# Second layer without the leading tokens behind its S5 input and rows, and S5 states stored from a copy

## Chip, cores and metric

The kernel runs on one core of a Trainium2 chip, as one launch. The metric is the device time of an execution in microseconds. The core's engines are TensorE (PE in the profile, PEld for its weight loads), VectorE (DVE), ScalarE (ACT), GpSimd (POOL) and SyncE (SP); all transfers run on 16 DMA engines, whichever engine's queue issues them.

## The reference

One inference step of a decoder with two layers over 280 columns: 16 learned leading tokens, 256 prompt tokens and 8 sample tokens (one step for each of 8 sequences with old states). The leading tokens are dropped from the result. All data are float32.

```python
for l in range(2):
    proj = rmsnorm(x) @ w_in[l]      # S5 input (512) | RWKV rows (1792) | two gates (1024 each)
    ya, xr, xi = s5_branch(proj[..., :512], ...)        # diagonal complex scan, GELU, GLU
    yb, s_fin, sh = rwkv7_branch(proj[..., 512:2304], ...)
    m = sigmoid(gate_a) * ya + sigmoid(gate_b) * yb
    x = x + m @ w_out[l]
    x = x + (swiglu(rmsnorm(x)) if l == 0 else moe(rmsnorm(x)))   # top 2 of 8 experts
y = rmsnorm(x)[:, 16:]
```

Besides y, the last S5 states, the RWKV states and the last projected rows of both layers are returned, for the prompt and for each sample sequence. A layer's scans need the leading tokens of that layer's S5 input and RWKV rows. In the second layer nothing else of these tokens reaches a result.

## The kernel before

Activations lie with the feature on the partitions and T = 280 columns (N_META = 16 leading ones, TP = 272 with the prompt, then NS = 8 samples). x, h and gate are [128, chunk, T]; each 128-wide output tile of a matrix product goes to one PSUM bank as 128 x 280. All weights come in one stream of 1 MB slots through a ring of seven, which SP refills in order as TensorE gives slots back (weights_used).

Each engine runs one program written out by hand, and engines meet by semaphores alone. For layer l TensorE's mix (L1051) does: the norm's sums; 12 tiles of RWKV rows; the S5 input matrices (b_turned, direct); the last two row tiles and four tiles of S5 input; then the S5 inputs (inputs), the low-rank products (lora), and the 16 gate tiles (proj_tile with n of at least CR + CA = 18), the later ones mixed with kk_sums, bonus_sums and four y5_tile calls. y5_tile makes the S5 output of one chunk from the scanned states xs by many small products; it shares one bank, so each waits for VectorE's y5_add of the one before. Then rwkv interleaves sixteen halves of the GLU (glu_half, 4 products each) with the chunked RWKV-7 solve. finish_rwkv (L1005 on) does the group norm, the eight w_bo tiles, the eight w_out tiles and the sums of the next norm. One float32 product appears in the records as two matmuls.

ScalarE evicts every projection tile (proj_out: identity for rows and S5 input, sigmoid for the gates). After the gate tile with n = 30 it runs the exponentials of the cumulative decay, the GELU and the last three sigmoids. The exponentials write beta and kr, which lie on the bytes of xs. VectorE runs the scan (scan), then the RWKV inputs with bonus_in at L1853, and y5_add.

POOL's queue stores the last S5 states: column 68 of xs (the prompt) and columns 69 to 76 (the samples), 9 floats in a run, 32 runs in each partition.

```python
pool.wait_ge(S["scan_done"], l + 1)
pool.dma_start(a["o_s5"][l], xs[:, :, :, NK:XW]).then_inc(S["s5_out"], 16)
pool.wait_ge(S["so_out"], CB * (l + 1))
```

and ScalarE waits for that store ahead of its exponentials (`ac.wait_ge(S["s5_out"], 16 * (l + 1))`). After the second layer's mixer come the routing and the eight experts (TensorE gets split float32 products, weights split by ScalarE and VectorE), then the last norm (norm with i = 4) and the store of y in four DMAs on SP's queue.

Of the kernel before, what the change touches and what calls it, by code (L numbers as in the profile page):

```python
# [8 lines left out]
ALU = mybir.AluOpType  # L9
# [135 lines left out]
def build(nc, a, debug=None):  # L145

    with ExitStack() as ctx:
# [37 lines left out]
        rstd = sb("rstd", [P, 2, T])  # L185
        wend = sb("wend", [P, CB, 1 + NCH + NS])
# [75 lines left out]
        names = ["x_in0", "x_in1", "ones_in", "first_in", "consts", "small_w", "s0_in", "shift_out", "s5_out", "rw_out", "y_stored",  # L262
# [64 lines left out]

        def quad(bank, n):
            return pools[bank][:, 0:256 * n].rearrange("p (f t) -> p f t", f=CB * n)
# [9 lines left out]
        def _(sp):  # L339
# [35 lines left out]
        def _(pool):  # L375
# [34 lines left out]
            for l in range(DEPTH):  # L410
# [16 lines left out]
                pool.dma_start(a["o_s5"][l], xs[:, :, :, NK:XW]).then_inc(S["s5_out"], 16)  # L427
# [17 lines left out]
        def _(pe):  # L445
# [20 lines left out]
            def norm(i):  # L466


                for c in range(DC):
                    pe.wait_ge(S["norm_sq"], DC * i + c + 1)  # L470
                    last = mm(pools[0][:, 0:T], ones[:], squares(i)[:, c, :], c == 0, c == DC - 1)
                    if c == 0 and i in (1, 3):
                        last.then_inc(S["weights_used"], 1)
                last.then_inc(S["norm_ps"], 1)

            def proj_tile(l, n, at):
# [16 lines left out]
                products(pools[n % 3][:, 0:T], [(w[:, j, k, :], h[:, k, :]) for k in range(DC)], "proj_ps",  # L493
# [71 lines left out]
            def glu_half(l, n, c):  # L565
# [14 lines left out]
                products(pools[bank][:, 0:T], [(w[:, n % 2, c, k, :], y5[:, k, :]) for k in range(CA)],  # L580
# [424 lines left out]
            def finish_rwkv(l):  # L1005
# [5 lines left out]
                for f in range(CB):  # L1011
                    mm(pools[f][:, 0:T], blk[:], o_t[:, f, :]).then_inc(S["gn_ps"], 1)
                for f in range(CB):
                    pe.wait_ge(S["o_sq"], CB * l + f + 1)
                    last = mm(pools[4][32 * f:32 * f + 32, 0:T], blk[:, 0:P:4], tmp[1][:, f, :])
                last.then_inc(S["gn_ps"], 1)
                pe.wait_ge(S["gn_dve"], (2 * CB + 1) * l + CB + 1)
                for f in range(CB):
                    q = slice(32 * f, 32 * f + 32)
                    mm(pools[4 + f][:, 0:T], spread[q, :], rstd[q, 1, :]).then_inc(S["gn_ps"], 1)  # L1020
                base = MIX_AT[l] + S_WIN + S_GLU
                for n in range(DC):
# [6 lines left out]
                    if n == 0:  # L1029
                        for k in range(CB):  # L1030
                            pe.wait_ge(S["gn_dve"], (2 * CB + 1) * l + CB + k + 2)
                            last = mm(pools[0][:, 0:T], w[:, 0, k, :], o_t[:, k, :], k == 0, k == CB - 1)
                        last.then_inc(S["bo_ps"], 1)
                    else:
                        products(pools[n % 4][:, 0:T], [(w[:, n % 4, k, :], o_t[:, k, :]) for k in range(CB)], "bo_ps",
# [4 lines left out]
                for n in range(DC):  # L1040
# [6 lines left out]
                    products(pools[4 + n % 4][:, 0:T], [(w[:, n % 2, k, :], gate[:, k, :]) for k in range(DC)], "wo_ps",  # L1047
# [232 lines left out]
        def _(ac):  # L1280
# [9 lines left out]
            def norm(i):  # L1290
# [3 lines left out]
                for c in range(DC):  # L1294
# [6 lines left out]
                    fn(squares(i)[:, c, :], x[:, c, :], ACT.Square).then_inc(S["norm_sq"], 1)  # L1301
# [5 lines left out]
                fn(rstd[:, 0, :], pools[0][:, 0:T], ACT.Sqrt, scale=1.0 / D, bias=eps[:, 0:1]).then_inc(S["norm_rt"], 1)  # L1307

            def proj_out(l, n):
# [6 lines left out]
                else:  # L1316
                    ins = fn(gate[:, n - CA - CR, :], src, ACT.Sigmoid)
# [15 lines left out]
            def mix(l):  # L1333
# [46 lines left out]
                ac.wait_ge(S["s5_out"], 16 * (l + 1))  # L1380
# [12 lines left out]
                for f in range(CB):  # L1393
                    ac.wait_ge(S["gn_dve"], (2 * CB + 1) * l + f + 1)
                    fn(tmp[1][:, f, :], o_t[:, f, :], ACT.Square).then_inc(S["o_sq"], 1)
                ac.wait_ge(S["gn_ps"], (2 * CB + 1) * l + CB + 1)
                fn(rstd[:, 0, :], pools[4][:, 0:T], ACT.Sqrt, scale=1.0 / N, bias=eps[:, 1:2]).then_inc(S["o_std"], 1)
# [6 lines left out]
            def glu_gate(l, n):  # L1404
# [4 lines left out]
                fn(glu_s[:, n % 2, :], pools[4 if n else 5][:, 0:T], ACT.Sigmoid).then_inc(S["glu_sig"], 1)  # L1409
# [253 lines left out]
        def _(dve):  # L1663
# [19 lines left out]
            def norm(i, gains, out):  # L1683
                dve.wait_ge(S["norm_rt"], i + 1)
                step(v.reciprocal(rstd[:, 1, :], rstd[:, 0, :]))  # L1685
                for c in range(DC):
                    ins = v.scalar_tensor_tensor(out=out[:, c, :], in0=x[:, c, :], scalar=gains[:, c:c + 1],  # L1687
                                                 in1=rstd[:, 1, :], op0=ALU.mult, op1=ALU.mult)
# [136 lines left out]
            def mix(l):  # L1825
# [70 lines left out]
                for f in range(CB):  # L1896
                    dve.wait_ge(S["gn_ps"], (2 * CB + 1) * l + f + 1)
                    stt(out=o_t[:, f, :], in0=pools[f][:, 0:T], scalar=-1.0 / N, in1=o_t[:, f, :],
# [5 lines left out]
                v.reciprocal(rstd[:, 1, :], rstd[:, 0, :]).then_inc(S["gn_dve"], 1)  # L1904
                for f in range(CB):
                    dve.wait_ge(S["gn_ps"], (2 * CB + 1) * l + CB + f + 2)
                    ins = stt(out=o_t[:, f, :], in0=o_t[:, f, :], scalar=col(l, "gn_g", f), in1=pools[4 + f][:, 0:T],
                              op0=ALU.mult, op1=ALU.mult)
                step(ins)
                for f in range(CB):  # L1910
                    ins = tt(o_t[:, f, :], o_t[:, f, :], bonus[:, f, :], ALU.add)
                step(ins)
                for f in range(CB):
                    tt(o_t[:, f, :], o_t[:, f, :], gg[:, f, :], ALU.mult).then_inc(S["gn_dve"], 1)  # L1914

                for n in range(DC):
                    dve.wait_ge(S["bo_ps"], DC * l + n + 1)
                    step(tt(gate[:, DC + n, :], gate[:, DC + n, :], pools[n % 4][:, 0:T], ALU.mult))
                    tt(gate[:, n, :], gate[:, n, :], gate[:, DC + n, :], ALU.add).then_inc(S["bo_out"], 1)
                for n in range(DC):  # L1920
                    dve.wait_ge(S["wo_ps"], DC * l + n + 1)
                    tt(x[:, n, :], x[:, n, :], pools[4 + n % 4][:, 0:T], ALU.add).then_inc(S["wo_out"], 1)
# [11 lines left out]
            def glu_out(l, n):  # L1934

                dve.wait_ge(S["glu_sig"], DC * l + n + 1)
                step(v.tensor_tensor(gate[:, n, :], gate[:, n, :], glu_s[:, n % 2, :], ALU.mult))
                dve.wait_ge(S["glu_value_ps"], DC * l + n + 1)
                v.tensor_tensor(gate[:, n, :], gate[:, n, :], pools[4][:, 0:T], ALU.mult).then_inc(S["glu_out"], 1)
# [554 lines left out]
OUTS = {"y": (P, DC, T), "o_shift": (DEPTH, P, CR, 1 + NS), "o_s5": (DEPTH, P, JT, 2, 1 + NS),  # L2494
# [3 lines left out]
def results(r):  # L2498
    y = r["y"].transpose(2, 1, 0).reshape(T, D)
# [5 lines left out]
    return (c(y[None, N_META:TP]), c(y[TP:, None]), c(s5[0, :, :1]), c(s5[1, :, :1]), c(rw[:, :1]), c(sh[:, :1]),  # L2505
# [17 lines left out]
```

## Time and profile before

| | |
|---|---|
| median of 3 runs | 2017.32 us (2012.21 to 2017.56) |
| profiled execution, own time | 2021.26 us |
| its span, first to last instruction | 2019.5 us |
| TensorE busy, mean granted clock | 96% of the span, 0.96 |
| VectorE, ScalarE, POOL busy | 66%, 48%, 2% |
| layer 0, its FFN, layer 1 up to its S5 inputs | 0 to 690 us |
| layer 1, gate tiles with scan and y5 | 690 to 783 us |
| layer 1, GLU, RWKV solve, tail, routing | 783 to 994 us |
| experts and combination | 994 to 2003 us |
| last norm and store | 2003 to 2019.5 us |

Times in the profile are microseconds from the span's start. A timeline row has start, duration, engine, line, operation and tiles (most of SBUF's tiles lie in one tensor, arena, and all PSUM tiles are called bank), the count of merged instructions (x16), and in brackets the engine's idle time ahead of it and what ended it. L447 is the helper through which every matmul is issued, L1282 that of every ScalarE operation. Ends of matmuls are modelled.

### The profile page before, as it was taken

How to read it: one execution, taken by the hardware profiler on the slowest of the kernel's cores; microseconds unless marked ns; L12 is line 12 of the kernel's file. 1: busy time of each engine (PE TensorE's matmuls, PEld its weight loads, DVE VectorE, ACT ScalarE, POOL GpSimd, SP SyncE). 2: the span in 40 equal slices, each digit the busy share in tenths (PEclk: the TensorE clock that was granted, in tenths of full speed). 3: DMA queues.
4: the chain of work that ended last, by engine and by line, in shares of the span. 5: the costliest groups of instructions: out<-in, count | busy, mean ns of one | idle time of the engine just before them, and what ended most of it. 6: DMA issues, size and time to landing. Idle time of an engine off the chain costs nothing.

```text
span 2019.5 us, 34327 instructions
## 1 busy us (share of the span) xinstructions
PE 1931.4 (96%) x14001; PEld 1600.4 (79%) x14001; DVE 1342.5 (66%) x1479; ACT 978.1 (48%) x957; POOL 44.9 (2%) x40
## 2 busy tenths in 40 slices
PE   8999998899999999998699999999999999999997
PEld 6876885799987777876588787887878878788775
DVE  7484344445534384353478888988888888888885
ACT  2232321344321213220377767768677776767763
POOL 0000000000000000000000000000000000000000
PEclk9989997999999899988699999999999999999998
DMA  8534005344443451015299999999999999999982
GB/s 333 140 67 89 2 3 211 137 172 175 174 139 112 106 97 54 2 57 198 85 346 378 356 377 353 365 380 358 371 366 372 367 362 377 360 368 365 407 333 86
DMA packets 69949, 474.75 MB, mean 235 GB/s; under 512 B 8721, under 2 KB 9905, under 8 KB 14617
## 3 DMA queue, kind: packets, MB, share of 16 engines
q1 hardware_dynamic: 64800, 451.33, 60.3%
q0 software_dynamic: 4736, 20.74, 3.7%
q8 instruction: 86, 1.41, 0.3%
q10 hardware_dynamic: 304, 1.08, 0.1%
q14 instruction: 23, 0.18, 0.0%
HBM read 463.92 MB, written 11.37 MB: 235 GB/s over the span
## 4 chain that ended last, share of the span: by engine, by line
PE 46%; ACT 2%; DVE 1%; DMA 1%; issue 1%; DVEq 0%; ACTq 0%; SPq 0%
PE bank L447 44%; ACT w_hi L1282 1%; PE bank L1235 1%; DMA ring<-wstream_dram 1%; PE bank L1161 0%; ACT he_hi L1282 0%; DVE he_lo L2297 0%; DVE w_lo L2344 0%; DMA arena<-tokens_dram,token_i 0%; PE bank L1171 0%; DVE arena L2291 0%; DVE arena L1687 0%; DVE x L2310 0%; DVE rstd L1685 0%; DVE y_lo L2304 0%
## 5 line engine op out<-in xcount | busy, mean ns | idle before, releaser
L2344 DVE TENSOR_TENSOR w_lo<-ring,w_hi 128x2048 fp32r<-128x2048 f32 x336 | 754.9, 2284 | 42.4 <-ACT w_hi L1282 41.1
L1282 ACT ACTIVATE w_hi<-ring 128x2048 fp32r<-128x2048 f32 x336 | 626.1, 1911 | 38.7 <-DMA ring<-wstream_dram 37.9
L447 PE MATMUL bank<-arena,ring 128*128 128x280 f32 (+1 forms) x1856 | 441.8, 401 | 18.9 <-DVE arena L1914 7.9
L447 PEld LDWEIGHTS bank<-arena,ring 128*128 128x128 f32 (+1 forms) x1856 | 341.4, 195 | 105.0 <-issue 21.4
L1282 ACT ACTIVATE arena<-bank 128x280 f32<-128x280 f32 (+8 forms) x292 | 131.7, 468 | 583.3 <-PE bank L447 550.3
L447 PE MATMUL bank<-w_hi,he_hi 128*128 128x512 f32 x896 | 361.8, 404 | 9.0 <-DVE he_lo L2297 8.5
L447 PE MATMUL bank<-w_lo,he_hi 128*128 128x512 f32 x896 | 354.1, 395 | 0.0
L447 PE MATMUL bank<-w_hi,he_lo 128*128 128x512 f32 x896 | 353.4, 394 | 0.0
L447 PEld LDWEIGHTS bank<-w_hi,he_hi 128*128 128x128 f32 x896 | 169.0, 189 | 50.2 <-issue 11.9
L447 PEld LDWEIGHTS bank<-w_hi,he_lo 128*128 128x128 f32 x896 | 168.9, 189 | 41.4
L447 PEld LDWEIGHTS bank<-w_lo,he_hi 128*128 128x128 f32 x896 | 169.4, 189 | 35.9
L447 PE MATMUL bank<-w_hi,at_hi 128*128 128x512 f32 x448 | 177.8, 397 | 0.4 <-DVE w_lo L2344 0.4
L447 PE MATMUL bank<-w_hi,at_lo 128*128 128x512 f32 x448 | 177.0, 395 | 0.0
L447 PE MATMUL bank<-w_lo,at_hi 128*128 128x512 f32 x448 | 175.2, 391 | 0.0
L447 PE MATMUL bank<-arena 64*64 64x64 f32 (+14 forms) x3920 | 160.4, 250 | 11.5 <-ACT arena L1282 5.4
L447 PEld LDWEIGHTS bank<-arena 64*64 64x64 f32 (+7 forms) x3920 | 135.2, 142 | 38.0 <-issue 19.0
L1680 DVE TENSOR_TENSOR w_lo<-ring,fw_hi 128x2048 fp32r<-128x2048 f32 x33 | 75.6, 2292 | 51.2 <-ACT fw_hi L1282 51.2
L447 PE MATMUL bank<-h_hi,fw_hi 128*128 128x280 f32 x352 | 104.0, 295 | 5.1 <-DVE h_lo L2182 5.1
L447 PE MATMUL bank<-h_lo,fw_hi 128*128 128x280 f32 x352 | 103.5, 294 | 0.0
L447 PE MATMUL bank<-h_hi,w_lo 128*128 128x280 f32 x352 | 103.3, 293 | 0.0
L447 PEld LDWEIGHTS bank<-w_hi,at_lo 128*128 128x128 f32 x448 | 84.1, 188 | 19.5
L447 PEld LDWEIGHTS bank<-w_lo,at_hi 128*128 128x128 f32 x448 | 84.3, 188 | 19.2
(276 smaller groups left out, 1783.4 us busy)
## 6 DMA issues: line engine op xcount, KB each, us to landing
ring<-wstream_dram SPq DMA_DIRECT2D x427, 1024.0 KB, 6.7
parts_dram<-zeros_dram POOLq DMA_DIRECT2D x1, 2112.0 KB, 14.0
s<-s_dram POOLq DMA_DIRECT2D x2, 1024.0 KB, 14.4
o_rw_dram<-s POOLq DMA_DIRECT2D x2, 1024.0 KB, 4.9
arena<-parts_dram POOLq DMA_DIRECT2D x2, 1024.0 KB, 11.7
x<-x_dram SPq DMA_DIRECT2D x2, 560.0 KB, 4.3
y_dram<-arena SPq DMA_DIRECT2D x4, 280.0 KB, 2.1
arena<-s_b_dram POOLq DMA_DIRECT2D x2, 512.0 KB, 6.3
```

The lines of the kernel that those rows point to most:

```text
L447: return nc.tensor.matmul(out, lhsT, rhs, start=start, stop=stop, **k)
L1235: last = nc.tensor.transpose(pools[2][:, b * P:(b + 1) * P], act_e[:, b * P:(b + 1) * P], ident[:])
L1282: return nc.scalar.activation(out, in_, func, **k)
L1680: v.tensor_tensor(w_lo[(FFN_AT + n) % RING], slot(FFN_AT + n), fw_hi[n % 4].bitcast(F32), ALU.subtract)\
L2344: v.tensor_tensor(w_lo[n % RING], slot(n), w_hi[n % HALVES].bitcast(F32), ALU.subtract)\
```

## The change

In layer 1 the gate tiles, the GLU, the group norm, w_bo, w_out, the residual add, the norm ahead of the routing and the last norm work on columns 16 to 279 alone (own(l), wide(l) = 264). The S5 input, the RWKV rows, the scans, y5, the GELU and the RWKV solve keep all 280. y is stored and returned without the leading tokens' columns. In both layers GpSimd copies the last S5 states to a tile of their own, s5_last (288 floats in each partition), and the store takes whole rows of it; ScalarE's exponentials wait for the copy (s5_copied) instead of the store.

```diff
+        s5_last = sb("s5_last", [P, JT, 2, 1 + NS])
...
+        def own(l):
+            return slice(N_META if l else 0, T)
+
+        def wide(l):
+            return T - own(l).start
...
-                sp.dma_start(a["y"][:, q], h[:, q]).then_inc(S["y_stored"], 16)
+                sp.dma_start(a["y"][:, q], h[:, q, N_META:T]).then_inc(S["y_stored"], 16)
...
                 pool.wait_ge(S["scan_done"], l + 1)
-                pool.dma_start(a["o_s5"][l], xs[:, :, :, NK:XW]).then_inc(S["s5_out"], 16)
+                if l:
+                    pool.wait_ge(S["s5_out"], 16 * l)
+                nc.gpsimd.tensor_copy(s5_last[:], xs[:, :, :, NK:XW]).then_inc(S["s5_copied"], 1)
+                pool.wait_ge(S["s5_copied"], l + 1)
+                pool.dma_start(a["o_s5"][l], s5_last[:]).then_inc(S["s5_out"], 16)
...
-                products(pools[n % 3][:, 0:T], [(w[:, j, k, :], h[:, k, :]) for k in range(DC)], "proj_ps",
+                q = own(l) if n >= CR + CA else slice(0, T)
+                products(pools[n % 3][:, 0:T - q.start], [(w[:, j, k, :], h[:, k, q]) for k in range(DC)], "proj_ps",
...
-                products(pools[bank][:, 0:T], [(w[:, n % 2, c, k, :], y5[:, k, :]) for k in range(CA)],
+                products(pools[bank][:, 0:wide(l)], [(w[:, n % 2, c, k, :], y5[:, k, own(l)]) for k in range(CA)],
...
-                    products(pools[4 + n % 4][:, 0:T], [(w[:, n % 2, k, :], gate[:, k, :]) for k in range(DC)], "wo_ps",
+                    products(pools[4 + n % 4][:, 0:wide(l)], [(w[:, n % 2, k, :], gate[:, k, own(l)]) for k in range(DC)], "wo_ps",
...
-                    fn(squares(i)[:, c, :], x[:, c, :], ACT.Square).then_inc(S["norm_sq"], 1)
+                    fn(squares(i)[:, c, own(i >= 3)], x[:, c, own(i >= 3)], ACT.Square).then_inc(S["norm_sq"], 1)
...
-                    ins = fn(gate[:, n - CA - CR, :], src, ACT.Sigmoid)
+                    ins = fn(gate[:, n - CA - CR, own(l)], pools[n % 3][:, 0:wide(l)], ACT.Sigmoid)
...
-                ac.wait_ge(S["s5_out"], 16 * (l + 1))
+                ac.wait_ge(S["s5_copied"], l + 1)
...
-OUTS = {"y": (P, DC, T), "o_shift": (DEPTH, P, CR, 1 + NS), "o_s5": (DEPTH, P, JT, 2, 1 + NS),
+OUTS = {"y": (P, DC, TM), "o_shift": (DEPTH, P, CR, 1 + NS), "o_s5": (DEPTH, P, JT, 2, 1 + NS),
```

The same slices stand in the group norm, w_bo, the elementwise steps on VectorE and ScalarE that go with these products, and in the norms with i of 3 and 4.

## Rows read from the trace of the kernel before

**Rows 1.** Stages: stretch, its length, each engine's busy time (instructions), PEclk, DMA share, GB/s
```profile
994.00:1886.00 892.00, 878.95 (x3919) 712.97 (x3920) 756.03 (x460) 645.55 (x457) 31.03 (x19) 0.99 0.95 362
...
912.00:938.00 26.00, 20.92 (x80) 16.07 (x77) 11.99 (x28) 0.00 (x0) 0.00 (x0) 0.82 0.58 230
...
2003.40:2019.50 16.10, 7.00 (x16) 4.92 (x16) 5.36 (x9) 4.50 (x10) 0.00 (x0) 0.61 0.19 73
```

**Rows 2.** Timeline of ScalarE, layer 1: two evictions of gate tiles
```profile
730.10 0.40 ACT L1282 ACTIVATE arena<-bank 128x280 f32<-128x280 f32 x1 [3.37 <-PE bank L447]
733.87 0.40 ACT L1282 ACTIVATE arena<-bank 128x280 f32<-128x280 f32 x1 [3.37 <-PE bank L447]
```

**Rows 3.** Timeline, layer 1: ScalarE's exponentials, its last sigmoid, the first GLU products
```profile
772.63 4.36 ACT L1282 ACTIVATE arena<-arena 128x1120 f32<-128x1120 f32 x4
...
782.23 0.40 ACT L1282 ACTIVATE arena<-bank 128x280 f32<-128x280 f32 x1 [0.51 <-PE bank L447]
...
782.69 4.04 PE L447 MATMUL bank<-arena,ring 128*128 128x280 f32 x16 [0.49 <-ACT arena L1282]
```

**Rows 4.** Timeline, layer 1: the state store's issue, VectorE beside it, TensorE's bonus_sums
```profile
729.31 2.30 DVE L1847 TENSOR_SCALAR arena<-arena,pv 128x280 f32<-128x280 f32 x4 [0.23 <-DVE arena L1813]
729.44 1.78 POOL L427 DMA_DIRECT2D o_s_dram<-arena  x1 [63.01 <-DVEq L1814]
...
731.54 1.18 DVE L1849 TENSOR_SCALAR arena<-arena,pv 128x280 f32<-128x280 f32 x4
...
734.11 1.77 DVE L1853 SCALAR_TENSOR_TENSOR arena<-arena,pv 128x280 f32<-128x280 f32 x4
...
737.45 2.05 PE L447 MATMUL bank<-arena,blk 128*128 128x280 f32 x8
```

**Rows 5.** Timeline of TensorE, layer 1: one GLU half; the first wait after 783 us
```profile
803.08 2.05 PE L447 MATMUL bank<-arena,ring 128*128 128x280 f32 x8
...
863.05 0.51 PE L447 MATMUL bank<-ring,arena 64*64 64x64 f32 x10 [0.79 <-DVE ring L2059]
```

**Rows 6.** Timeline, layer 1's tail: group norm sums, reciprocal, w_bo, w_out
```profile
903.33 5.03 PE L447 MATMUL bank<-arena,blk 128*128 128x280 f32 x16 [1.58 <-DVE arena L2066]
...
908.99 1.90 DVE L1904 RECIPROCAL rstd<-rstd 128x280 f32<-128x280 f32 x1 [0.75 <-ACT rstd L1282]
...
916.23 17.76 PE L447 MATMUL bank<-arena,ring 128*128 128x280 f32 x64 [3.97 <-DVE arena L1914]
...
935.11 30.42 PE L447 MATMUL bank<-arena,ring 128*128 128x280 f32 x128 [1.12 <-DVE arena L1919]
```

**Rows 7.** Timeline of ScalarE: evictions beside the y5 tiles, layers 0 and 1
```profile
152.50 0.40 ACT L1282 ACTIVATE arena<-bank 128x280 f32<-128x280 f32 x1 [5.26 <-PE bank L447]
...
171.90 0.40 ACT L1282 ACTIVATE arena<-bank 128x280 f32<-128x280 f32 x1 [10.33 <-PE bank L447]
178.54 0.40 ACT L1282 ACTIVATE arena<-bank 128x280 f32<-128x280 f32 x1 [6.24 <-PE bank L447]
...
743.31 0.40 ACT L1282 ACTIVATE arena<-bank 128x280 f32<-128x280 f32 x1 [5.26 <-PE bank L447]
...
757.62 0.40 ACT L1282 ACTIVATE arena<-bank 128x280 f32<-128x280 f32 x1 [6.51 <-PE bank L447]
```

**Rows 8.** Timeline: TensorE in layer 0's y5 tiles, VectorE ahead of layer 1's first y5_add
```profile
165.88 0.32 PE L447 MATMUL bank<-arena 128*32 128x76 f32 x3 [2.09 <-issue]
...
750.00 0.69 DVE L1820 SCALAR_TENSOR_TENSOR arena<-arena,pv,bank 128x272 f32<-128x272 f32 x1 [6.13 <-remote]
```

**Rows 9.** DMA: ring loads (139:166; 700:729) with us to landing; instruction packets (737:741; 753:757)
```profile
ring<-wstream_dram SPq DMA_DIRECT2D x2, 1024.0 KB, 17.9
...
ring<-wstream_dram SPq DMA_DIRECT2D x2, 1024.0 KB, 4.8
...
q8 instruction: 1, 0.02, 9.5%
...
q8 instruction: 1, 0.02, 1.5%
```

More of the change, by code:

```diff
@@ L470, in norm @@
                     pe.wait_ge(S["norm_sq"], DC * i + c + 1)
-                    last = mm(pools[0][:, 0:T], ones[:], squares(i)[:, c, :], c == 0, c == DC - 1)
+                    last = mm(pools[0][:, 0:wide(i >= 3)], ones[:], squares(i)[:, c, own(i >= 3)], c == 0, c == DC - 1)
                     if c == 0 and i in (1, 3):
@@ L1019, in finish_rwkv @@
                     q = slice(32 * f, 32 * f + 32)
-                    mm(pools[4 + f][:, 0:T], spread[q, :], rstd[q, 1, :]).then_inc(S["gn_ps"], 1)
+                    mm(pools[4 + f][:, 0:wide(l)], spread[q, :], rstd[q, 1, own(l)]).then_inc(S["gn_ps"], 1)
                 base = MIX_AT[l] + S_WIN + S_GLU
@@ L1031, in finish_rwkv @@
                             pe.wait_ge(S["gn_dve"], (2 * CB + 1) * l + CB + k + 2)
-                            last = mm(pools[0][:, 0:T], w[:, 0, k, :], o_t[:, k, :], k == 0, k == CB - 1)
+                            last = mm(pools[0][:, 0:wide(l)], w[:, 0, k, :], o_t[:, k, own(l)], k == 0, k == CB - 1)
                         last.then_inc(S["bo_ps"], 1)
                     else:
-                        products(pools[n % 4][:, 0:T], [(w[:, n % 4, k, :], o_t[:, k, :]) for k in range(CB)], "bo_ps",
+                        products(pools[n % 4][:, 0:wide(l)], [(w[:, n % 4, k, :], o_t[:, k, own(l)]) for k in range(CB)], "bo_ps",
                                  release=n == 4)
@@ L1408, in glu_gate @@
                 ac.wait_ge(S["glu_ps"], DC * l + n + 1)
[L1409 removed]
+                fn(glu_s[:, n % 2, 0:wide(l)], pools[4 if n else 5][:, 0:wide(l)], ACT.Sigmoid).then_inc(S["glu_sig"], 1)
             def s_tokens(l, j):
@@ L1684, in norm @@
                 dve.wait_ge(S["norm_rt"], i + 1)
-                step(v.reciprocal(rstd[:, 1, :], rstd[:, 0, :]))
+                q = own(i >= 3)
+                step(v.reciprocal(rstd[:, 1, q], rstd[:, 0, q]))
                 for c in range(DC):
-                    ins = v.scalar_tensor_tensor(out=out[:, c, :], in0=x[:, c, :], scalar=gains[:, c:c + 1],
-                                                 in1=rstd[:, 1, :], op0=ALU.mult, op1=ALU.mult)
+                    ins = v.scalar_tensor_tensor(out=out[:, c, q], in0=x[:, c, q], scalar=gains[:, c:c + 1],
+                                                 in1=rstd[:, 1, q], op0=ALU.mult, op1=ALU.mult)
                     ins.then_inc(S["h_ready"], 1)
@@ L1897, in mix @@
                     dve.wait_ge(S["gn_ps"], (2 * CB + 1) * l + f + 1)
-                    stt(out=o_t[:, f, :], in0=pools[f][:, 0:T], scalar=-1.0 / N, in1=o_t[:, f, :],
+                    stt(out=o_t[:, f, own(l)], in0=pools[f][:, 0:wide(l)], scalar=-1.0 / N, in1=o_t[:, f, own(l)],
                         op0=ALU.mult, op1=ALU.add).then_inc(S["gn_dve"], 1)
```

34 lines of the change are left out of this document (17 added, 17 removed).

## The prediction

> **What bounds the kernel now.** I read the share of busy time first, then the stages, then the chain. TensorE is busy nearly all of the time, and half of the execution is the expert stage: from 994 to 1886 us it is busy 878.95 of 892 us at the full granted clock [rows 1]. The change touches nothing there, and the weight ring of that stage is refilled as TensorE gives slots back, so the stage moves as a block: whatever the second layer's mixer saves ahead of it is saved at the end. The question is therefore how much earlier TensorE finishes three stretches: the projections of layer 1 (686 to 783 us), its GLU and RWKV stretch (783 to 903), and its tail up to the routing (903 to 972); then the final norm, and for the stored states the same place in both layers. In these stretches the reader is to look for two things: a steady rhythm of ScalarE's evictions, which means that TensorE sets the pace, and places where the rhythm breaks.
>
> **Part 1, the columns: what a tile is worth.** In layer 1 the gate tiles of the projection come out at an even 3.77 us (730.10 to 733.87), each with ScalarE idle 3.37 us for TensorE [rows 2]. Such a tile is 8 products of 280 columns. With 264 columns it is worth 16/280 less if time goes by columns: 3.77 x 0.0571 = 0.215 us. Bounds: nothing, if a fixed cost per product filled the time, and 0.215 us. I take the upper end, since TensorE has no gap in the rhythm.
>
> Projection: sixteen tiles, 16 x 0.215 = 3.45 us. Not all of it passes on. At the end of this stretch ScalarE is waited for: its chain of exponentials, GELU and three sigmoids starts after the thirteenth of the sixteen tiles, and it ends at 782.63; there it waited 0.51 us for the last tile, and TensorE then 0.49 us for it [rows 3]. With the chain's own length unchanged (the GELU still runs over all columns) TensorE gets 13 x 0.215 = 2.80 us from the earlier start and the 0.51 us of ScalarE's wait: 3.3 us. The last tiles' gain beyond that becomes waiting for ScalarE.
>
> One wait may take some back. bonus_sums waits for VectorE's product (L1853), which ends at 734.11 + 1.77 = 735.88; TensorE arrives at 737.45 [rows 4]. It will arrive 8 x 0.215 = 1.72 us earlier, at 735.73, while VectorE starts its scan only 0.2 us earlier (one gate tile lies ahead of it). So the slack of 1.57 us is used up and 0 to 1.3 us may be waited; I take 0.3, which is the difference plus a hand-over. Behind it on TensorE stand the four y5 tiles and the rest of the projection.
>
> GLU: sixteen half tiles of 4 products, 2.05 us each in the record [rows 5], lose 0.117 us each: 1.87 us. Up to 863.05 us TensorE waits for nobody in this stretch (there the first wait, 0.79 us for VectorE, stands) [rows 5], and the last half tile is over by then, so nearly all of it passes on. The half tiles lie between small products that need results of ScalarE and VectorE, and a few of these could now come late: bounds 0 and 1.87, I take 1.7.
>
> Tail: the sums for the group norm (8 products, 5.03 us), one reciprocal (1.90 us), the w_bo tiles (17.76 us) and the w_out tiles (30.42 us) follow one another without anything beside them that is longer [rows 6]. 55.1 us x 0.0571 = 3.15 us; the reciprocal of the next norm and its last product add about 0.15: 3.3 us. The elementwise steps on VectorE between them are left out, they are worth hundredths each.
>
> Final norm: 7.00 us of TensorE [rows 1] x 0.0571 = 0.40, its reciprocal as above 0.11: 0.5 us. The store of y now takes rows out of a tile with the first 16 columns left out, two runs per partition instead of one; no row shows such a store, I take 0 and bounds of -0.1 and +0.3 us, from its few us behind the last product.
>
> Columns together: 3.3 + 1.7 + 3.3 + 0.5 - 0.3 = 8.5 us.
>
> **Part 2, the stored states.** Before, one POOL DMA per layer stores 288 numbers of each partition in runs of 9, straight from the scan's tile, for which ScalarE's exponentials have to wait. Now GpSimd copies them, and the DMA stores whole rows; the exponentials wait for the copy. That wait costs nothing: POOL issues at 729.44 [rows 4], and the exponentials start at 772.63 in the same layer [rows 3]; behind the copy POOL has only its own store and those of the RWKV states, which nobody in the layer waits for. What the old store does to others is the point. After it, the rhythm breaks in both layers: with y5 tiles in between, ScalarE's evictions come 6.64 us apart (171.90 to 178.54), but in layer 0 it is 19.40 us from 152.50 to 171.90, where two periods are 13.28, so 6.12 us are lost; in layer 1 it is 14.31 us from 743.31 to 757.62, 1.03 us lost [rows 7]. In that place TensorE stands idle 2.09 us for nothing that the profile shows (165.88), and VectorE 6.13 us for a signal called remote [rows 8]. At the same time two ring loads land after 17.9 us in layer 0, against 4.8 us in the 29 us ahead of layer 1's store, and instructions too come slowly: one block of the instruction queue right after layer 1's store, 9.5% of 16 engines for 4 us, is 6.1 us in flight, against 1.5%, 1.0 us, for one later [rows 9]. So I take it that the many small writes hold up the DMA engines, and with them the instructions that the dense y5 products eat fastest. Nothing else is due in these stretches, VectorE waits there, so the 7.15 us come back if the cause is right. Bounds: 0 and 7.15, I take 7.15, since all signs stand in the same 30 us of both layers.
>
> The Trainium skill speaks against this. Its page "Runtime: NRT & Kernel Launch", section "Instruction fetch mechanics", says that an engine fetches its next page of instructions by a DMA queue of its own while it executes the present one, and that this stays mostly hidden. By that rule slow blocks would not stop TensorE, and the sum would be the columns' 8.5 us alone; that is rival A.
>
> GpSimd's copy: no row shows one. The nearest rows are POOL's own issue, 1.78 us, and VectorE beside it: four products with a column took 2.30 us while POOL issued, four of the same size 1.18 us right after [rows 4]. So POOL's work costs VectorE up to 1.12 us now. I bound the copy's cost to VectorE by -1.1 us (a shorter issue) and +1.8 us (a second such block), and take 0, because it hits VectorE where it is 1.57 us ahead of TensorE; the 0.3 us above covers what is left.
>
> **The sum.** The profiled execution took 2021.26 us, with 2019.5 of span. 2021.26 - 8.5 - 7.15 = 2005.6 us. It lies 3.94 us over the median of the runs shown, 2017.32; they spread by 5.35 us, so a part of what the profiled one lost may be missing in others.
>
> **The rivals.**
> A. The old store is not what breaks the rhythm (something else in these 30 us does, or fetching is not what stops TensorE): 2021.26 - 8.5 = 2012.8. For it: the 2.09 us bear no name, and the block with 6.1 us is in layer 1, where less is lost. Against: the store is the only thing that this place of both layers has and the rest of the mixer lacks. 0.14.
> B. The interleaved stretches are bound by their hand-overs, not by TensorE's columns, so that projection and GLU give nothing: 7.15 + 3.3 + 0.5 = 10.95 us, 2010.3. For it: the 0.49 us wait and the thin slack at bonus_sums; against: no recorded wait up to 863. 0.13.
> C. The runs without profile are the better base and lose as much in the store: 2017.32 - 15.65 = 2001.7. For it: the median; against: their spread, which looks like a loss that comes and goes. 0.08.
> D. Slower: the granted clock. TensorE idles before the w_bo tiles, and from 912 to 938 us the mean grant is 0.82, that is, a part at the lower of the two levels (1.2 of 2.4 GHz); in the last 16 us it is 0.61, and there 8 products take 7.00 us instead of 3.77 [rows 1, 2]. If with less work per tile the grant rose later, each further tile at the lower level would cost 3.23 us: from five on the gain is gone, from seven on it is slower by more than the bound. With all eight w_out tiles it would be 2005.6 + 25.8 = 2031.4. Against: the tiles shrink by 6%, the idle time ahead of them doesn't grow. 0.04.
> That the change doesn't do what it says would show as A or B.
>
> **How the numbers follow.** Forecast 2005.6 us with 0.61, A 0.14, B 0.13, C 0.08, D 0.04. A measurement of this kernel tells about 0.3% from no change, 6.05 us, so 2011.3 is the border: forecast, B and C lie under it (0.82), A within (0.14), D over (0.04). The range takes in A, B and C: the upper end is A, 2013.0; the lower end goes 2.2 us under C, less than half of the runs' spread: 1999.5.
>
> **What would show it.** ScalarE's gate evictions 3.55 to 3.57 us apart in layer 1, and still 3.77 in layer 0: the columns. Ring loads landing in 5 to 7 us after the store, y5 periods of 6.64 us without break in layer 0 and 6.43 in layer 1: the store. ScalarE no longer waiting for the last projection tile, and TensorE up to 0.7 us for ScalarE. A wait of TensorE for VectorE's L1853 line under 1.3 us. The w_out stretch (eight tiles and the norm's products under their end) near 28.7 us instead of 30.42. It would be wrong if the y5 stretch of layer 0 still lost 6 us, or if the grant in the tail fell under 0.82.

## The result, and the profile after

| | before | after |
|---|---|---|
| device time, median of five runs | 2017.32 us | 2002.89 us |
| profiled execution, and its span | 2021.26 us, 2019.5 us | 2002.89 us, 2001.1 us |
| TensorE busy | 1931.45 us | 1918.1 us |
| mean granted TensorE clock | 0.960 | 0.961 |

The changed kernel takes 0.9931 of the time before, with a 95% interval of 0.9913 to 0.9949. In a second comparison on another chip (the last experiments) it was 0.9929, 0.9913 to 0.9945. The forecast was 2005.6 us. One of the six executions of the kernel with the columns alone, an experiment further down, took 3808 us and is not in its ratio.

**Where the time went.** The program of ScalarE is the same in both kernels, so the start of one and the same ScalarE instruction can be compared. The table has the length of the stretches between eight such instructions, in us, worked out from their starts. The second trace of after is from that later comparison.

| stretch (times of the trace before) | before | after | after, second trace |
|---|---|---|---|
| start to an early row tile of layer 1 (608.17) | 608.17 | 602.48 | 603.84 |
| to the first low-rank product (697.97) | 89.80 | 86.75 | 86.74 |
| gate tiles and y5, to the last sigmoid (782.23) | 84.26 | 79.86 | 79.90 |
| GLU and RWKV (862.31) | 80.08 | 76.67 | 76.67 |
| end of RWKV, to the group norm (903.77) | 41.46 | 44.63 | 42.35 |
| tail and routing, to the first expert (999.65) | 95.88 | 93.22 | 92.56 |
| experts, to the last one's last pieces (1964.69) | 965.04 | 964.51 | 963.61 |
| to the root of the last norm (2011.03) | 46.34 | 44.66 | 45.06 |
| to the end | 8.47 | 8.32 | 8.27 |

Six rows are shorter by 1.7 us or more, one is longer, two hardly change. The reader can see that the saving is not all of one kind: the second row has almost no cut product in it, and the fifth row changes between two traces of the same kernel.

**The gate tiles.** The timeline of ScalarE in after, layer 1; it answers to [rows 2, 3]. Columns: start, duration, engine, line, operation, and in brackets the idle time before it with what ended it.

```profile
720.12 0.39 ACT L1294 ACTIVATE arena<-bank 128x264 f32<-128x264 f32 x1 [3.17 <-PE bank L458]
723.68 0.39 ACT L1294 ACTIVATE arena<-bank 128x264 f32<-128x264 f32 x1 [3.17 <-PE bank L458]
...
745.55 0.39 ACT L1294 ACTIVATE arena<-bank 128x264 f32<-128x264 f32 x1 [6.04 <-PE bank L458]
751.98 0.39 ACT L1294 ACTIVATE arena<-bank 128x264 f32<-128x264 f32 x1 [6.04 <-PE bank L458]
...
760.11 4.36 ACT L1294 ACTIVATE arena<-arena 128x1120 f32<-128x1120 f32 x4
...
768.51 0.97 ACT L1294 ACTIVATE arena<-bank 128x264 f32<-128x264 f32 x3
```

Gate tiles come 3.56 us apart instead of 3.77, y5 periods are 6.43 us without a break, and ScalarE's last three sigmoids run in one piece: the 0.51 us for the last tile is gone. TensorE now waits for it instead, 0.48 us, as the timeline of TensorE shows, together with the tail (it answers to [rows 4, 6]):

```profile
727.04 2.05 PE L458 MATMUL bank<-arena,blk 128*128 128x280 f32 x8
...
769.53 3.83 PE L458 MATMUL bank<-arena,ring 128*128 128x264 f32 x16 [0.48 <-ACT arena L1294]
...
889.94 5.57 PE L458 MATMUL bank<-arena,blk 128*128 128x264 f32 x16 [1.57 <-DVE arena L2079]
...
902.69 17.42 PE L458 MATMUL bank<-arena,ring 128*128 128x264 f32 x64 [3.80 <-DVE arena L1927]
921.19 28.72 PE L458 MATMUL bank<-arena,ring 128*128 128x264 f32 x128 [1.08 <-DVE arena L1932]
```

bonus_sums (727.04) bears no wait. The w_out stretch takes 28.72 us, 30.42 before. The w_bo stretch gained only 0.34 us, and the group norm's sums are slower than before although their tiles are smaller: the granted clock was lower there, of which more below.

**The store.** POOL and VectorE in layer 1 (timelines; against [rows 4]), then the ring loads and the store in layer 0 (DMA issues from 141 to 168 us, with KB and us to landing; against [rows 9]):

```profile
720.46 0.43 POOL L436 COPY s_last<-arena 128x288 f32<-128x288 f32 x1 [59.46 <-DVEq L1827]
721.19 0.55 POOL L438 DMA_DIRECT2D o_s_dram<-s_last  x1 [0.30 <-POOL s_last L436]
```

```profile
719.08 1.26 DVE L1826 TENSOR_TENSOR arena<-arena 128x1056 f32<-128x1056 f32 x1
720.57 1.31 DVE L1860 TENSOR_SCALAR arena<-arena,pv 128x280 f32<-128x280 f32 x4 [0.23 <-DVE arena L1826]
721.80 1.18 DVE L1862 TENSOR_SCALAR arena<-arena,pv 128x280 f32<-128x280 f32 x4
```

```profile
ring<-wstream_dram SPq DMA_DIRECT2D x3, 1024.0 KB, 4.7
```

The copy takes 0.43 us, the issue 0.55 instead of 1.78, and VectorE's four products beside it 1.31 instead of 2.30. Ring loads land in 4.7 us (the median of three) where they took 17.9 (the median of two). Layer 0, whose products are not cut, shows the store alone. ScalarE's evictions there, against [rows 7]:

```profile
153.50 0.40 ACT L1294 ACTIVATE arena<-bank 128x280 f32<-128x280 f32 x1 [5.26 <-PE bank L458]
160.15 0.40 ACT L1294 ACTIVATE arena<-bank 128x280 f32<-128x280 f32 x1 [6.24 <-PE bank L458]
166.79 0.40 ACT L1294 ACTIVATE arena<-bank 128x280 f32<-128x280 f32 x1 [6.24 <-PE bank L458]
173.43 0.40 ACT L1294 ACTIVATE arena<-bank 128x280 f32<-128x280 f32 x1 [6.24 <-PE bank L458]
```

Three periods of 6.64 us, 19.93 in all, where before it was 178.54 - 152.50 = 26.04 us: 6.1 us came back.

In layer 1, where 1.03 us were lost, the break came about in another way. TensorE and VectorE at the first y5 tile, before and then after:

```profile
743.20 2.77 PE L447 MATMUL bank<-arena 32*32 32x204 f32 x88
750.87 2.74 PE L447 MATMUL bank<-arena 32*32 32x204 f32 x88 [0.94 <-DVE arena L1822]
```

```profile
732.58 2.74 PE L458 MATMUL bank<-arena 32*32 32x204 f32 x88
735.39 0.71 DVE L1833 SCALAR_TENSOR_TENSOR arena<-arena,pv,bank 128x272 f32<-128x272 f32 x1 [1.26 <-PE bank L458]
```

After, VectorE's addition starts 0.07 us behind the tile's last product (735.32). Before, it started at 750.00 [rows 8], 4.0 us behind (745.97), for a signal called remote, and TensorE waited 0.94 us for it. Such waits of VectorE or ScalarE stand in four traces, those of before and of three experiments below, all with short runs in y5 or the GLU, and in no other. What delays the signal is not shown.

### The profile page after: what moved, and what is told of

It reads as the page before. It is cut to its first block, busy times and chain, and to the rows that moved or that the text cites. A ratio compares the mean times of both kernels' runs of the same rounds, so it can differ in the third digit from the quotient of the medians.

```text
span 2001.1 us, 34330 instructions
## 1 busy us (share of the span) xinstructions
PE 1918.1 (96%) x14001; PEld 1597.7 (80%) x14001; DVE 1339.2 (67%) x1479; ACT 976.9 (49%) x957; POOL 43.9 (2%) x42
## 4 chain that ended last, share of the span: by engine, by line
PE 48%; ACT 1%; DVE 1%; issue 1%; DMA 0%; DVEq 0%; ACTq 0%
PE bank L458 46%; PE bank L1247 1%; ACT w_hi L1294 1%; PE bank L1173 0%; DVE he_lo L2310 0%; DMA arena<-tokens_dram,token_i 0%; ACT he_hi L1294 0%; PE bank L1183 0%; DVE arena L2304 0%; DVE arena L1700 0%; DVE w_lo L2357 0%; DVE rstd L1698 0%; DVE y_lo L2317 0%; DVE arena L2328 0%; DVE x L2323 0%
## 5 line engine op out<-in xcount | busy, mean ns | idle before, releaser
L2357 DVE TENSOR_TENSOR w_lo<-ring,w_hi 128x2048 fp32r<-128x2048 f32 x336 | 754.9, 2285 | 42.0 <-ACT w_hi L1294 40.8
L458 PE MATMUL bank<-arena,ring 128*128 128x280 f32 (+2 forms) x1856 | 430.3, 395 | 18.7 <-DVE arena L1927 7.8
L1294 ACT ACTIVATE arena<-bank 128x280 f32<-128x280 f32 (+9 forms) x292 | 131.3, 467 | 573.7 <-PE bank L458 536.0
```

Source lines behind the costliest of these rows:

```text
L458: return nc.tensor.matmul(out, lhsT, rhs, start=start, stop=stop, **k)
L1294: return nc.scalar.activation(out, in_, func, **k)
L2357: v.tensor_tensor(w_lo[n % RING], slot(n), w_hi[n % HALVES].bitcast(F32), ALU.subtract)\
```

## The experiments

The theory: two independent savings, products cut by 16/280 where TensorE sets the pace, and a store whose 36-byte runs delay other transfers, among them TensorE's instructions. Rivals: A, the store isn't the cause; B, the interleaved stretches don't follow the columns; D, the granted clock in the tail takes the gain back. All times below are compared with runs of the kernel before on the same chip. Its median was 2016.3 us beside the first four kernels, 2017.75 beside the next four and 2017.16 beside the last two. The ratios and intervals are those on record with the runs. They are not the quotients of the two medians and differ from them by up to some 0.06%, 1.2 us.

### The two parts, each alone

The store alone is the kernel before with these lines in both layers, and ScalarE waiting for s5_copied:

```diff
-pool.dma_start(a["o_s5"][l], xs[:, :, :, NK:XW]).then_inc(S["s5_out"], 16)
+if l:
+    pool.wait_ge(S["s5_out"], 16 * l)
+nc.gpsimd.tensor_copy(s5_last[:], xs[:, :, :, NK:XW]).then_inc(S["s5_copied"], 1)
+pool.wait_ge(S["s5_copied"], l + 1)
+pool.dma_start(a["o_s5"][l], s5_last[:]).then_inc(S["s5_out"], 16)
```

> The kernel before with the second part of the change alone, in both layers: GpSimd copies the last S5 states, whole rows are stored, ScalarE waits for the copy. If the old store breaks TensorE's rhythm (the forecast's step): 4 to 7 us less than before, ScalarE's y5 evictions 6.64 us apart without a break in layer 0 (153.5 to 180), ring loads there landing in 5 to 7 us. If it does not (rival A): within 2 us of before, and the break of about 6 us still stands in layer 0.

Measured: 2011.72 us, 0.9972 of before (0.9960 to 0.9984). The y5 evictions of layer 0 stand at 152.62, 159.27, 165.91, 172.56, without a break. The store is a cause, and A is refuted.

The columns alone are the changed kernel with the old store put back (the diff above, reversed).

> The kernel before with the first part of the change alone: the second layer's gate tiles, GLU, group norm, w_bo, w_out and the last norm over 264 columns; the old store stays. By the forecast's sum 8.5 us less than before, gate evictions of layer 1 at 3.56 us, and the y5 break of some 6 us still in layer 0. If hand-overs bound the interleaved stretches (rival B): 3.8 us less. Together with the run that has only the store, the two savings should add up to that of the whole change, 14.4 us.

Measured: 2006.76 us, 0.9949 (0.9931 to 0.9967), and gate tiles 3.56 us apart. TensorE waits for VectorE ahead of bonus_sums here, as the forecast had feared, 0.74 us:

```profile
733.98 2.15 PE L453 MATMUL bank<-arena,blk 128*128 128x280 f32 x8 [0.74 <-DVE arena L1861]
```

The y5 break of layer 0 is there, but in this trace it is small: one period of 8.89 us, 2.25 us lost, where the trace of before lost 6.1.

```profile
162.12 0.40 ACT L1289 ACTIVATE arena<-bank 128x280 f32<-128x280 f32 x1 [6.24 <-PE bank L453]
171.01 0.40 ACT L1289 ACTIVATE arena<-bank 128x280 f32<-128x280 f32 x1 [8.49 <-PE bank L453]
177.66 0.41 ACT L1289 ACTIVATE arena<-bank 128x280 f32<-128x280 f32 x1 [6.24 <-PE bank L453]
```

By the medians the two savings are 4.6 and 9.5 us, 14.1 together, and the whole change saved 14.4. By the ratios they are 0.28 and 0.51%, against 0.69% for the whole. Within the intervals the parts add up. The loss by the old store is not a fixed amount: it differs between executions.

### Is it the length of the runs?

The kernel with the store alone, with a tenth, unused float behind every nine of the copy, so that the DMA again reads runs of 36 bytes; ScalarE waits for the copy only.

```diff
-s5_last = sb("s5_last", [P, JT, 2, 1 + NS])
+s5_last = sb("s5_last", [P, JT, 2, 2 + NS])
...
-nc.gpsimd.tensor_copy(s5_last[:], xs[:, :, :, NK:XW]).then_inc(S["s5_copied"], 1)
+nc.gpsimd.tensor_copy(s5_last[:, :, :, 0:1 + NS], xs[:, :, :, NK:XW]).then_inc(S["s5_copied"], 1)
...
-pool.dma_start(a["o_s5"][l], s5_last[:]).then_inc(S["s5_out"], 16)
+pool.dma_start(a["o_s5"][l], s5_last[:, :, :, 0:1 + NS]).then_inc(S["s5_out"], 16)
```

> As the run with the store alone, but the copy has a spare float behind every nine, so that the DMA still reads runs of 36 bytes; ScalarE waits for the copy alone, as in the change. If the length of the runs is what costs: as before within 2 us, with the y5 break of some 6 us in layer 0. If it was ScalarE's wait for the store, or reading the scan's own tile: 4 to 7 us less, as with whole rows.

Measured: 2014.77 us, 0.9993 (0.9980 to 1.0007), as before. DMA issues from 138 to 168 us of this kernel, then from 138 to 165 us of the one with whole rows (number, KB, median us to landing):

```profile
ring<-wstream_dram SPq DMA_DIRECT2D x3, 1024.0 KB, 8.4
o_s_dram<-s_last POOLq DMA_DIRECT2D x1, 144.0 KB, 21.6
```

```profile
ring<-wstream_dram SPq DMA_DIRECT2D x3, 1024.0 KB, 4.7
o_s_dram<-s_last POOLq DMA_DIRECT2D x1, 144.0 KB, 5.0
```

The same 144 KB from the same place need 21.6 us in short runs and 5.0 in rows, and the ring loads 8.4 against 4.7. Neither ScalarE's wait nor the scan's own tile is the cause; the runs are. In this trace 3.6 us were lost in layer 0's y5 stretch and 1.3 in layer 1's.

### Without the store

The store and ScalarE's wait for it are left out, so this kernel doesn't return the last S5 states.

> The kernel before without the store of the last S5 states (these outputs are left out), so neither the copy nor the wait of ScalarE for the store. The floor of the second part. If whole rows are free: as the run with the store alone, that is 3 to 6 us less than before and within 2 us of 2011.7. If the whole-row store or the copy still costs: clearly under that run, by 2 us or more.

Measured: 2011.67 us, 0.9966 (0.9954 to 0.9978). The kernel with the whole-row store had 0.9972. The intervals overlap (on two chips), so copy and whole rows cost nothing that can be measured, and the second part takes all that there was to take.

### What do the short runs delay?

Two kernels keep the short runs and issue them elsewhere; their diffs are against the kernel with the short runs from a copy. In the first, the store waits for two finished GLU tiles; TensorE is in small products there and no ring load is under way.

```diff
 nc.gpsimd.tensor_copy(s5_last[:, :, :, 0:1 + NS], xs[:, :, :, NK:XW]).then_inc(S["s5_copied"], 1)
+pool.wait_ge(S["glu_out"], DC * l + 2)
 pool.wait_ge(S["s5_copied"], l + 1)
```

> As the run with 36-byte runs from a copy, but the store is issued some 30 us later, when two GLU tiles are finished: TensorE runs dense small products there and no weight loads are under way. The y5 stretch should run through without a break. If slow instruction blocks are what stops TensorE: idle time of 2 to 6 us without a named cause in the GLU stretch of a layer, and a total within 2 us of before. If late weight loads were what stopped it: no such idle time, and 4 to 7 us less than before.

Measured: 2021.07 us, 1.0030 (1.0013 to 1.0046): slower than before, by 4.8 us of the medians. The y5 stretch of layer 0 is whole (153.04 to 172.97, 19.93 us), and the break stands in the GLU now. TensorE in layer 0, with the store issued at 205.45:

```profile
216.36 1.17 PE L453 MATMUL bank<-arena 16*16 16x16 f32 x21 [0.29 <-issue]
217.46 0.66 PE L745 MATMUL bank<-ident,arena 128*128 128x128 f32 x4
217.96 1.93 PE L453 MATMUL bank<-arena,ring 128*128 128x280 f32 x5
220.90 1.75 PE L453 MATMUL bank<-arena,ring 128*128 128x280 f32 x3 [1.02 <-issue]
222.59 2.83 PE L453 MATMUL bank<-ring 64*64 64x64 f32 x48
```

The first idle time stands between products of one and the same group, the second between eight products of one tile with its operands in place. What is under way then is one instruction block and the end of the store. The block's share of 16 engines, from 215 to 220 us of this kernel, then from 212 to 217 us of the one with whole rows, where the same block is due:

```profile
q8 instruction: 1, 0.02, 5.5%
```

```profile
q8 instruction: 1, 0.02, 1.1%
```

That is 5.5% x 16 x 5 = 4.4 us in flight against 0.9 us. In layer 1 the trace has 0.62 and 1.85 us of idle time near the same place without a name. So what TensorE lacks here is not weights. That it is instructions was argued from the slow block, and the traces bear it out in layer 0. TensorE starts again 1.2 us after the end of this block (219.70). In y5, counted from the eviction at 152.50 [rows 7] and its like, the first instruction block starts 2.5 to 3.2 us later in the nine traces without short runs there, and 8.8 to 10.1 us later in the three with them (before, columns alone, short runs from a copy), though TensorE itself was at most some 2 us behind by then. TensorE's longest idle time there, 1.7 to 2.1 us, ends 1.3 to 1.5 us after that block. So what counts there is a block that starts 6 to 7 us late, not one that takes long: those three took 0.9 to 2.9 us. In layer 1 of the present kernel it does not fit: TensorE goes on at 806.77, before the next block (806.90 to 808.92). There the cause stays open.

The stop can cost more than itself, as the stages of this kernel show (as in [rows 1]; the column after POOL's is the granted clock):

```profile
212.00:218.60 6.60, 6.17 (x95) 5.12 (x94) 0.97 (x3) 1.18 (x2) 0.00 (x0) 1.00 0.05 2
218.60:225.40 6.80, 5.78 (x55) 3.89 (x55) 0.27 (x1) 1.35 (x3) 0.00 (x0) 0.50 0.01 2
225.40:232.20 6.80, 6.80 (x127) 5.92 (x126) 2.50 (x6) 2.38 (x5) 0.00 (x0) 1.00 0.01 2
```

Around the idle time the clock is at the lower level, 1.2 GHz, for 6.8 us; the kernel with whole rows keeps 2.4 GHz there. Layer 1 has the same from 805.7 to 812.5 us.

In the second kernel the short runs go out behind the RWKV states, where TensorE has large products and the tail's weights are on their way.

```diff
-pool.wait_ge(S["s5_copied"], l + 1)
-pool.dma_start(a["o_s5"][l], s5_last[:, :, :, 0:1 + NS]).then_inc(S["s5_out"], 16)
...
 pool.dma_start(a["o_rw"][l][:, :, 0, :], z_last).then_inc(S["rw_out"], 16)
+pool.wait_ge(S["s5_copied"], l + 1)
+pool.dma_start(a["o_s5"][l], s5_last[:, :, :, 0:1 + NS]).then_inc(S["s5_out"], 16)
```

> 36-byte runs from a copy as before, but issued behind the RWKV states' stores, where TensorE runs the tail's large products of 128x280 with weight loads under way. If the short runs only hurt where TensorE eats its instructions fast: 3 to 6 us less than before, no unnamed idle time of TensorE in the tail of either layer. If they hurt by late weight loads too: waits of TensorE for the ring in a tail, and a total within 2 us of before.

Measured: 2021.03 us, 1.0015 (1.0003 to 1.0027). I had thought this the harmless place; it is not. The waits of TensorE from 898 to 945 us (total, times, longest), and its w_bo tiles:

```profile
PE bank L452 <- DMA ring<-wstream_dram: 9.8, 1, 9.8
```

```profile
920.45 16.86 PE L452 MATMUL bank<-arena,ring 128*128 128x280 f32 x64 [9.77 <-DMA ring<-wstream_dram]
```

TensorE waits 9.8 us for weights, and 10.1 us in layer 0, where before it waited some 4 us for VectorE [rows 6]. Seven ring loads take 21.3 us to land by their median (895 to 923 us), against 11.1 in the kernel with whole rows at the same place. So the short runs delay weights too, and here the wait bears their name. What TensorE lacks first depends on where it is.

### The tail alone

The changed kernel, with gate tiles and GLU over 280 columns again.

```diff
-q = own(l) if n >= CR + CA else slice(0, T)
+q = slice(0, T)
...
-products(pools[bank][:, 0:wide(l)], [(w[:, n % 2, c, k, :], y5[:, k, own(l)]) for k in range(CA)],
+products(pools[bank][:, 0:T], [(w[:, n % 2, c, k, :], y5[:, k, :]) for k in range(CA)],
...
```

> The whole change, but the second layer's gate tiles and GLU over all 280 columns again: the store, and 264 columns in group norm, w_bo, w_out and the last norms. By the forecast 3.8 us (3.3 and 0.5) under the run with the store alone, so about 2007.9, and the remaining 5 us of the columns belong to gates and GLU. If the tail gives nothing, because the granted clock rises later there (rival D's place): 2011 to 2012.

Measured: 2007.06 us, 0.9952 (0.9938 to 0.9967), 4.7 us under the store alone by the medians, on another chip, and 4.6 under the kernel without the store, on the same one; 3.8 had been expected. The intervals just overlap. The w_out stretch between the same two ScalarE instructions is 28.02 us here and in every trace with the cut, 29.71 in every trace without it (29.70 once).

### The clock in the tail, and a further cut

The changed kernel once more, and beside it a version with more of the leading tokens taken out of layer 1: four chunks of four tokens less in each y5 tile and its addition, the GELU over 264 columns, and no outputs of the first RWKV chunk.

```diff
-src = xs[:, j, c, 0:NK] if i < 3 else xs[:, j, c, 1:XW]
+src = xs[:, j, c, k0:NK] if i < 3 else xs[:, j, c, 1 + k0:XW]
...
-fn(y5[:, aa, :], y5[:, aa, :], ACT.Gelu_apprx_tanh)
+fn(y5[:, aa, own(l)], y5[:, aa, own(l)], ACT.Gelu_apprx_tanh)
...
```

> The whole change and two more cuts of the leading tokens in the second layer: the y5 tiles, their additions and the GELU over 264 columns, and no RWKV outputs of the first chunk of 16. Estimate: four y5 tiles of 2.87 us x 4/68 = 0.7 us, and some 1 us for 32 small products: 1.7 us under the whole change, about 2001.2. If hand-overs set the pace there: within 0.5 us of the whole change.

> The changed kernel once more, beside the one with the two further cuts, for a second trace of it. Its first trace has 10 us more at the lower clock between 862 and 903 us of the old time than the trace with the columns alone, so that its stretch from the RWKV end to the group norm took 44.6 us against 40.7. If the shorter tiles cause that (rival D's place): again 44 us or more. If it comes and goes: between 40.6 and 44.8, and the time 0.65 to 0.75% under before.

> The whole change with y5, its additions and GELU over 264 columns and without the RWKV outputs of the first chunk, on the same chip as the changed kernel. From its trace: the y5 and GELU stretch 36.05 us against 36.40 with the change alone, the RWKV stretch the rest of some 1.5 us: 1 to 2 us under the changed kernel, or 0 if the clock takes it.

Measured: the further cut 2001.88 us (0.9918, 0.9903 to 0.9933) and 2001.12 us (0.9918, 0.9901 to 0.9934); the changed kernel beside the second one 2002.11 us (0.9929, 0.9913 to 0.9945). In the traces the stretch from an eviction among the y5 tiles to the last sigmoid is 35.85 us instead of 36.40. It is the fastest version of all, by 1.0 us of the medians, but the intervals overlap, so this is not settled.

The stretch from RWKV's end to the group norm, by stages: the changed kernel, its second trace, the kernel without the store and all columns, and the columns alone, one line each.

```profile
845.70:890.40 44.70, 40.82 (x820) 35.52 (x820) 22.44 (x52) 9.64 (x21) 1.45 (x2) 0.75 0.09 29
```

```profile
847.10:889.50 42.40, 38.53 (x820) 33.36 (x821) 22.35 (x52) 9.63 (x20) 1.45 (x2) 0.84 0.09 31
```

```profile
851.10:895.80 44.70, 40.69 (x820) 35.51 (x821) 22.35 (x52) 9.64 (x20) 1.46 (x2) 0.77 0.08 29
```

```profile
852.80:893.50 40.70, 36.87 (x820) 31.75 (x821) 22.31 (x52) 9.68 (x21) 1.45 (x2) 0.87 0.09 32
```

The same 820 products take 36.9 to 40.8 us of TensorE, and the length goes with the grant: 44.7 us at 0.75 and 0.77, 42.4 at 0.84, 40.7 at 0.87. Of these four the two longest are one trace with the cut and one without, so nothing here says that the cut lowers the clock. From the second of the group norm's squares to the first eviction of w_out, where rival D had its place, the six traces with the cut take 32.6 to 33.0 us and those without it 33.3 us or more. Rival D is not seen.

## Why the prediction was right, step by step

**The base: 4 us too high.** The sum started from 2021.26 us, 3.94 above the median, as the profile of one execution. In three later comparisons before had medians of 2016.3 to 2017.75. What made that execution long is partly in its trace: 7.1 us lost to the store in the two y5 stretches, where other traces with short runs there lost 2.25 (columns alone) and 4.9 us; and two stretches at the lower clock. One, at 819 us, comes under GLU. The other is from 682 to 689 us, where layer 1's S5 input products and a gate tile ran at half speed, 19.1 us at a grant of 0.82; after has the same work in 15.7 us at 1.00:

```profile
679.70:698.80 19.10, 16.93 (x337) 15.41 (x337) 0.62 (x2) 5.12 (x13) 0.00 (x0) 0.82 0.27 98
```

```profile
674.30:690.00 15.70, 13.59 (x336) 12.71 (x336) 0.56 (x2) 5.05 (x13) 0.00 (x0) 1.00 0.27 102
```

Some 3 us of the difference between the two traces are this, and belong to no term of the sum. The kernel with the store alone and one of the two traces of the further cut have that slow stretch too, the nine other traces have not. It comes and goes, and what decides it was not found.

**The store: right cause, the size taken from a heavy sample.** 7.15 us were taken, the upper bound, read from one execution. Timed it is 4.6 us by the medians, 0.28% by the ratio (0.16 to 0.40%), and 6.1 us or 0.34% (0.22 to 0.46%) with the store left out. 7.15 us are 0.35%, so the intervals do not exclude them, but three traces lost 2.25, 4.9 and 7.1 us. The mechanism holds in its main part: no break in y5, ring loads at 4.7 us, a break that moves with the store. Of the 6.1 us in layer 0, 4.4 are time that TensorE lost in the first two y5 tiles, and 1.7 a gate tile at the lower clock (5.73 us at 166.13, where it takes 4.04). The forecast was too simple in layer 1. The block of 6.1 us that it named is there, but there TensorE did not stop for it: it waited for VectorE. Rival A is refuted as far as the store goes. The sentence of the Trainium skill on which it leaned ("Runtime: NRT & Kernel Launch", section "Instruction fetch mechanics": fetching stays mostly hidden) agrees with the nine traces without short runs in y5, where TensorE does not stop; beside the short runs, where a block starts 6 to 7 us late and TensorE stops for 1.7 to 2.1 us, it does not, and the measurement decides. What the Trainium skill says on its page "DMA: Bandwidth & Descriptors", section "Queues, rings and completion order", that an engine takes turns between its queues a whole packet at a time, agrees with these traces, since blocks and ring loads are slow while the many small pieces are in flight; no run here shows the turns themselves.

**The copy: right.** Taken as 0 with bounds of -1.1 and +1.8; VectorE's products beside it were 1.0 us shorter (1.31 for 2.30), near the lower bound, and for the reason named, POOL's shorter issue. That also removed the wait at bonus_sums for which 0.3 us had been set aside: VectorE ended its product at 726.15 (724.38 + 1.77), TensorE came at 727.04. With the columns alone, where the long issue stays, the wait is there, 0.74 us.

**Gate tiles: right.** Forecast 3.3 us. From the second gate tile's eviction (713.12 of the old time) to the last sigmoid it is 68.08 us in each of the five traces with gate tiles over 280 columns and no short runs there, and 65.09 and 65.10 in the two of after: 3.0 us. Eleven tiles give 2.35 of them, 0.214 each, and the end of ScalarE's wait 0.64, where 0.51 had been forecast. The two tiles ahead of it lie where the clock changes between traces (697.97 to 713.12 takes 14.0 to 15.2 us), so their 0.4 us cannot be read. ScalarE's wait turned into 0.48 us of TensorE's, as forecast (up to 0.7).

**GLU: right, and B is refuted.** Forecast 1.7. The stretch is 78.39 us with the store alone, and in two more traces with the GLU over 280 columns, and 76.67 in both traces of after: 1.72. In the two traces of the table above it shrinks by 3.4, but 1.7 of that is a slow stretch that before happened to have at 819 us.

**Tail: right in kind, the first half too large.** w_out gave 29.71 - 28.02 = 1.69 of the 1.74 us forecast. From the second of the group norm's squares to the first of the w_out evictions it is 32.6 to 33.0 us in the traces with the cut and 33.3 to 34.5 without (the one that waited for weights left out): a gain between 0.3 and 1.9 where 1.5 had been taken, with the clock deciding. The warning sign of the forecast, a grant under 0.82 in the tail, did appear, if barely. In the 26 us that end 1.6 us ahead of the first eviction of w_out, where before had 0.82, both traces of after have 0.80, and the store alone 0.87. (From 882 to 918 us after even has 0.68, but that takes in 8 us of the end of RWKV, which changes by 4 us between traces that do the same work there.) By the forecast's own words this would have made it wrong, and yet from those squares on every trace with the cut is shorter than every one without. It was the wrong sign to set.

**Last norm: 0.5 forecast.** The stretch to its root is 44.9 to 47.3 us in the six traces without the cut and 44.7 to 45.1 in the six with it. Three of the six without it are over 46, with a mean grant of 0.85 to 0.86; all others have 0.89. At the same grant the gain is about 0.5 us at most and not separable from zero. Whether the cut also helps to avoid the slow case is not settled.

The columns together were forecast at 8.5 and timed at 9.5 by the medians (0.51%, 0.33 to 0.69%); stretch by stretch the traces give 3.0 to 3.4 + 1.72 + 1.69 + 0.3 to 1.9 + 0 to 0.5, that is 6.7 to 9.2 us. So the forecast came out 2.7 us high: its base was 4 us high and the columns by the medians 1 us low, while the store, 1 to 2.5 us too large, worked against that. The terms were right in kind; that their errors partly cancel is luck. Rival C's number, 2001.7, was nearer than the forecast (1.2 us off), and its first half, the median as the better base, was right; its second half, the same loss in the store, is not borne out by the medians.

## What to carry to other kernels

The price of a transfer can lie in what else is in flight, and not in its own length: a store of 144 KB in each layer, which TensorE never waits for, cost up to 7 us in the kernel before, because its 36-byte runs delayed other transfers: weights for certain, instructions in all likelihood. Gathering such pieces into whole rows first, here by an idle engine in 0.43 us, is worth more than moving the store, since each of the three places tried had something to delay. Another queue for the short runs was not tried. And a loss read from one execution is a sample: where it comes and goes, the median is the base, and the loss in one trace is one draw (here 2.25, 4.9 and 7.1 us).

## What the runs showed of the hardware

- The same store of 144 KB from SBUF landed after 21.6 us in runs of 36 bytes (19.2 us in the tail), and after 2.0 to 5.2 us in rows of 1152 bytes. Beside the short runs ring loads of 1 MB had medians of 8.4 and 17.9 us instead of 4.7 (y5, layer 0). An instruction block started 6 to 7 us late there, and single blocks took 4.4 and 6.1 us instead of 1.
- Idle time of TensorE without a name was followed by a grant of 0.50 in some traces and not in others. In the trace of before it is so for 3.4 us from 166.8, just behind the 2.09 us of [rows 8]. With 2.02 us at the same place (short runs from a copy) and 1.66 us (columns alone) the grant stayed at 1.00. Before:

```profile
152.50:166.80 14.30, 11.19 (x195) 7.42 (x194) 3.44 (x5) 0.81 (x2) 0.00 (x0) 1.00 0.69 73
166.80:170.20 3.40, 3.40 (x9) 2.50 (x8) 2.09 (x3) 0.00 (x0) 0.00 (x0) 0.50 0.66 178
170.20:178.60 8.40, 8.40 (x115) 5.77 (x117) 3.97 (x4) 0.47 (x2) 0.00 (x0) 1.00 0.15 57
```

- Stretches at the lower clock of 3.4 to 20 us change their number and place between executions. The end of RWKV took 44.63 and 42.35 us in two traces of the changed kernel, and 40.6 to 44.8 in all ten traces that do the same work there. That is as much as the cut of the tail is worth.
- GpSimd's copy of 128x288 floats out of runs of nine took 0.43 us. VectorE's four products that started beside it took 1.31 us, 0.13 more than the four of the same size behind them.
